# Square root and reciprocal in place of logarithm and exponential in five row norms of a two-block network

## The reference

```python
def rms_norm(x, gain):
    xf = x.astype(f32)
    y = xf * lax.rsqrt(jnp.mean(xf * xf, axis=-1, keepdims=True) + EPS)
    return (y * gain.astype(f32)).astype(x.dtype)

        h = rms_norm(x, norm_mix[l]) * (1.0 + sc_m) + sh_m      # first block, mixer
        hf = rms_norm(x, norm_ffn[l]) * (1.0 + sc_f) + sh_f     # first block, SwiGLU
    return rmsnorm(h, norm_final)                               # end of the second block
```

## Time and profile before

| what | value |
|---|---|
| runs | 4066.3, 4072.77, 4072.88 us, median 4072.77 |
| profiled execution | 4076.04 us, its span 4074.2 us |
| PE busy | 3920.8 us, 96% of the span |
| DVE busy | 2182.6 us, 54% |
| ACT busy | 814.5 us, 20% |
| POOL busy | 787.0 us, 19% |
| chain that ended last | PE 90%, DVE 4%, ACT 3%, issue 2%, DMA 1% |
| table loads at L1734 | 11 of 1283 ns |
| mean granted clock of PE | 0.987 |

### The profile page before, as it was taken

The page is one execution under the profiler, slowest core; times in us unless marked ns, Lnnn a source line. Parts: engine busy times, 40 slices in busy tenths (PEclk is TensorE's granted clock), DMA queues, the critical chain, the costliest instruction groups (busy, mean ns, idle before and its releaser), DMA issues.

```text
span 4074.2 us, 46405 instructions
## 1 busy us (share of the span) xinstructions
PE 3920.8 (96%) x17592; PEld 2913.7 (72%) x17592; DVE 2182.6 (54%) x3669; ACT 814.5 (20%) x1429; POOL 787.0 (19%) x656
## 2 busy tenths in 40 slices
PE   7999989999999999999999999999999999999998
PEld 3444478755555555665888886888789999778886
DVE  2144467534446431334556675554698888556546
ACT  2243355320100013542110101000131111110002
POOL 0038723110003100000003001130044444121300
PEclk9999999999999999999999999999999999999999
DMA  5244300012121121102332232222222222122321
GB/s 177 90 166 148 132 4 1 32 52 62 51 62 49 65 72 42 42 32 72 93 82 86 81 93 73 93 92 89 80 73 67 68 70 63 52 91 85 98 83 62
DMA packets 377174, 307.86 MB, mean 76 GB/s; under 512 B 9424, under 2 KB 345680, under 8 KB 376912
## 3 DMA queue, kind: packets, MB, share of 16 engines
q1 hardware_dynamic: 377040, 306.03, 24.1%
HBM read 303.90 MB, written 2.10 MB: 75 GB/s over the span
## 4 chain that ended last, share of the span: by engine, by line
PE 90%; DVE 4%; ACT 3%; issue 2%; DMA 1%; SPq 0%; POOL 0%; POOLq 0%; DVEq 0%; ACTq 0%
PE ps_lin L848 17%; PE ps_lin L721 10%; PE ps_lin L785 9%; PE ps_d L848 9%; PE ps_lin L1554 6%; PE ps_d L785 5%; PE ps_c L848 4%; PE ps_lin L704 4%; PE ps_d L704 3%; PE ps_lin L990 3%; PE ps_c L785 2%; PE ps_d L1340 2%; PE ps_lin L1221 2%; PE ps_lin L1208 1%; PE ps_c L704 1%
## 5 line engine op out<-in xcount | busy, mean ns | idle before, releaser
L848 PE MATMUL ps_lin<-arena,ring 128*128 128x256 f32 (+1 forms) x832 | 226.2, 425 | 1.1 <-DVE arena L2316 1.1
L3272 POOL TENSOR_TENSOR hid_in<-arena 128x256 f32<-128x256 f32 (+1 forms) x60 | 50.5, 870 | 879.9 <-PE ps_d L848 879.9
L848 PE MATMUL ps_lin<-hid_in,mixed 128*128 128x384 f32 (+1 forms) x704 | 205.4, 445 | 14.1 <-ACT hid_in L1748 13.8
L785 PE MATMUL ps_lin<-arena,ring 128*128 128x256 f32 (+1 forms) x864 | 214.1, 401 | 0.0
L2340 DVE TENSOR_TENSOR arena<-ring 128x1024 f32<-128x1024 f32 x84 | 123.0, 1464 | 168.7 <-PE ps_d L785 139.8
L721 PE MATMUL ps_lin<-mixed,ring 128*128 128x512 f32 (+1 forms) x544 | 210.4, 549 | 0.1
L3147 POOL TENSOR_TENSOR rstd<-rstd,square 128x512 f32<-128x512 f32 (+1 forms) x50 | 74.9, 1497 | 688.5 <-ACT square L1726 687.7
L848 PEld LDWEIGHTS ps_lin<-arena,ring 128*128 128x128 f32 x832 | 158.1, 190 | 64.4 <-issue 3.8
L848 PE MATMUL ps_d<-arena,mixed 128*128 128x384 f32 (+1 forms) x704 | 196.7, 432 | 0.0
L785 PEld LDWEIGHTS ps_lin<-arena,ring 128*128 128x128 f32 x864 | 164.1, 190 | 41.2 <-issue 0.2
L848 PE MATMUL ps_lin<-hid_in,arena 128*128 128x256 f32 x832 | 188.6, 380 | 3.6 <-DVE arena L2343 3.6
(11 more groups left out here) (501 smaller groups left out, 7991.1 us busy)
## 6 DMA issues: line engine op xcount, KB each, us to landing
ring<-in_ffn_w_in SPq DMA_DIRECT2D x88, 512.0 KB, 4.6
resid<-in_ada_w SPq DMA_DIRECT2D x20, 2048.0 KB, 7.9
ring<-in_mlp_w_up SPq DMA_DIRECT2D x64, 512.0 KB, 4.5
ring<-in_mlp_w_down SPq DMA_DIRECT2D x64, 512.0 KB, 4.4
ring<-in_attn_w_qkv SPq DMA_DIRECT2D x64, 512.0 KB, 4.8
ring<-in_ffn_w_out SPq DMA_DIRECT2D x32, 512.0 KB, 4.1
ring<-in_even_w_in SPq DMA_DIRECT2D x28, 512.0 KB, 5.0
ring<-in_sc_w_in SPq DMA_DIRECT2D x24, 512.0 KB, 4.9
```

Of the source, the lines that this page charges most:

```text
L785: last = mm(prod[i - 1], lhs[:, j, :], rhs(p), start=(g == j == 0), stop=(g == G - 1 and j == np_ - 1))
L848: last = mm(out, lhs[:, j, :], rhs[:, j, :], start=(j == 0), stop=(j == 3))
L3272: tt(sums[p][i], u, v, op).then_inc(s.u_hp, 1)
```

## The change

A tuple `ROOT` names the norms that are changed. For those, ScalarE loads the table of the square root ahead of its wait, takes the square root of mean + eps in one instruction that counts up `n_rs`, and is done. VectorE, once it has waited for `n_rs`, takes the reciprocal of all columns of the row in place, waits for its end, and goes on with the products as before. In mix0 this stands at the place of the old wait. "ffn0b" and "ffn1b" are not in `NORMS`; the other five of the tuple are. The six of `LATE` keep logarithm and exponential.

```diff
+ROOT = ("mix0", "ffn0", "ffn0b", "mix1", "ffn1", "ffn1b", "final")
...
             def rstd_of_norm(name, width):
-                logs()
+                act.preload_act_table(ACT.Sqrt if name in ROOT else ACT.Ln)
                 act.wait_ge(s.n_mm, MM_COUNT[name])
                 r = RS[:, 0, 0:width]
+                if name in ROOT:
+                    fn(r, psc[:, 0:width], ACT.Sqrt, bias=m["eps"], scale=1.0 / D).then_inc(s.n_rs, 1)
+                    return
                 chain(fn(r, psc[:, 0:width], ACT.Ln, bias=m["eps"], scale=1.0 / D))
...
+            def inverse(name, u, v):
+
+                dve.wait_ge(s.n_rs, NORMS.index(name) + 1)
+                chain(dve.reciprocal(RS[:, 0, u:v], RS[:, 0, u:v]))
+
             def norm(name, width, gains, strassen=None):
...
                 dve.wait_ge(s.n_rs, n + 1)
+                if name in ROOT:
+                    inverse(name, 0, width)
                 for k in range(KD):
...
             mod_scale(0, 0)
-            dve.wait_ge(s.n_rs, 1)
+            inverse("mix0", 0, T)
             for k in (0, 1):
                 scaled(k)
```

## The result

| | before | after |
|---|---|---|
| median | 4070.49 us (15 runs, 4065.58 to 4074.82) | 4078.41 us (15 runs, 4076.84 to 4080.83) |
| span of the first profiled execution | 4074.2 us | 4075.5 us |
| PE busy | 3920.8 us | 3909.9 us |
| DVE busy, instructions | 2182.6 us, 3669 | 2196.9 us, 3674 |
| ACT busy, instructions | 814.5 us, 1429 | 804.9 us, 1419 |

The ratio is 1.0021, with a 95% interval from 1.0013 to 1.0029: 7.9 us slower (by the interval, 5 to 12). The forecast was 16.1 us slower. The direction was right; the size was twice too large. A second comparison, at another time, gave 4080.86 against 4073.13 us, ratio 1.0027 (1.0017 to 1.0036).

The account below looks back on a forecast made before the run. TensorE was taken to bound the kernel; mix0 +4.2, ffn0 and mix1 +3.8 each, ffn1 +2.3, final +2.1 make +16.1 on the median 4072.77: 4088.9 us. Overall range 4065 to 4098; slow division by itself 4082 to 4104.

Parts of the forecast that it names:

- What bounds the kernel: Whole kernel: 90% of the chain that ended last lies on TensorE; an edit elsewhere counts only where TensorE stands still.
- What is removed: Table load and exponential behind the logarithm: saves 2.13 us at ffn0 and mix1, 1.69 ffn1, 1.92 final, nothing at mix0.
- The reciprocal: Added on VectorE at five norms: 7.5 ns a column, 5.91 us for 768 columns, 3.99 for 512.
- the early rows: 24 one-column reciprocals early in the run, median 164 ns, taken to mean 5.5 to 12 ns a column.
- The late one-column rows: 32 later one-column reciprocals, 153 ns, implying 1 ns a column; judged the weaker witness, as one column can hide division steps.
- mix0: First norm: reciprocal of 5.91 us pushes the next transpose, which had 1.73 us to spare: +4.2 us, nothing given back.
- It falls already with the waits of before, so a longer wait costs nothing more at four of the norms.: TensorE's granted clock after waits: no added cost at four norms; at mix0 one more low stretch would cost 2.3 us.
- One column a step: Rival: reciprocals at all five norms take 0.95 or 0.69 us, -4.6 us in all, 4068.2 us; chance 0.20.
- rival 2: Reciprocals at the five norms cost 2.5 to 5 ns a column, giving 4072 to 4081 us; chance 0.06.
- The drain: Rival: the removed table load hides a drain, so four norms each gain more than 1.283 us; 4063 us; chance 0.02.
- the load that comes back: Rival: root gets its own load behind the wait, 1.283 us at four norms, +5.1 us; 4094 or 4073 us; chance 0.02.
- The signs of being wrong: Reciprocal under 5 ns a column; TensorE's first product at ffn0 moving unlike VectorE's; clock at 0.50 longer behind longer waits.

Follow-up runs that it names:

- the three pairs of traces: The unedited kernel before and the changed kernel, each profiled three times and paired in order; spans before 4074.2, 4070.1, 4070.7 us, after 4075.5, 4078.7, 4079.7 us.
- The first pair of traces: The first profiled execution of the unedited kernel before, and that of the changed kernel; spans 4074.2 and 4075.5 us.
- the second traces of both kernels: Repeat profiles without any edit of the kernel before and the changed kernel; spans 4070.1 and 4078.7 us, medians 4071.97 and 4080.86 us.
- all fourteen traces: Three traces of the kernel before, three of the changed kernel, and one of each follow-up variant; medians of the variants run from 4049.94 to 4078.76 us.

## Why the prediction was wrong, point by point

- **What bounds the kernel.** Right. At ffn0 a delay of VectorE's first product of 2.90 us is a delay of TensorE's first matmul of 2.90.
- **What is removed.** Right within 0.1: the root costs what the logarithm did; the hop from ScalarE to VectorE is 0.10 us (root done at 881.26, reciprocal at 881.36), not 0.03. The load is worth its 1.283 us, as the kernel with only the load taken away shows.
- **The reciprocal: the term that was mis-sized.** I took 7.5 ns a column, measured are 6.26. It lies within the 5.5 to 12 of the early rows, at their lower end. On the sum that is 1.24 x 3.33 = 4.1 us: 16.1 becomes 12.0. It is the first of two steps that failed. The figure from the Trainium skill, "VectorE: DVE Perf Modes", by which a column would take an estimated 8.3 ns, is too high here; that a column of a reciprocal costs several times one of a product, the trace confirms. The late one-column rows (1 ns) were the weaker witness, as I said; that a single column hides the division's steps, no run tests. The choice of 7.5 within the bounds was a guess.
- **mix0.** +4.2 was said, and with 6.26 ns it would have been 3.3. It is 4.0, 4.6 and 3.5 in the three pairs of traces. That +4.2 lies among these is luck: the reciprocal is 0.96 us shorter than forecast, and the cover and VectorE's arrival at the row come out 0.2 to 1.4 us worse. The spare 1.73 us belongs to traces in which TensorE does the 16 products at its lower clock; one of the three has 0.56. The cover was read from a single execution.
- **"It falls already with the waits of before, so a longer wait costs nothing more at four of the norms."** This is the second step that failed. It costs nothing more: at mix1 the same matmuls from TensorE's first product on take 15.65 us in the first trace of before and 15.59 in that of after. But the time at the lower clock came to lie otherwise in four places, which gave 4.75 us back, and I had looked for a loss only: the forecast put this term at nothing. 12.9 less 4.75 is 8.2, and 7.9 was measured. The nearness is in part luck, since the three pairs of traces give back 4 to 5 us between ffn0 and final and mix0 costs 3.5 to 4.6. (The first pair of traces has 1.3 between the spans because of what the clock did ahead of ffn0, which differs by up to 4.6 us between traces of the same code.)
- **The rivals.** One column a step (0.20) is refuted by 6.26 ns, and so is rival 2, 2.5 to 5 ns (0.06), though the time measured lies in its band of 4072 to 4081. The drain is refuted by the kernel with only the load taken away, the load that comes back by the six loads left at the exponential's line. The time is inside my overall range but below the 4082 at which the forecast's own range began.
- **The signs of being wrong.** None of the three came: a column costs more than 5 ns, TensorE's first product at ffn0 moved by the same 2.90 us as VectorE's, and behind the longer wait the clock stayed low for less long, 7.9 us for 10.7. No sign was named for a clock that gives time back.

Open stays why the low stretch at ffn0 lasts 17.1 us with a wait of 9.57 us (one extra reciprocal) and 13.7 with one of 9.54 (root at ffn0 and ffn1), and by what a change at ffn0 decides how the clock falls 400 and 1800 us later. That it does is seen in traces only; the times of these kernels are too close to confirm it one by one.

## What to carry to other kernels

Before a reciprocal is moved from a row of statistics to all columns, ask for its price at that width: here 6.26 ns a column, so 768 columns cost 4.95 us to save 2.1 of table load and exponential. The load itself can go without anything in its place, if one table with both functions is asked for by name; look then also for the loads further on that this makes superfluous. And a term of a few us on TensorE's path is only as good as the clock behind it: take more than one trace, and compare windows cut from the same matmul to the same matmul.

## What the runs showed of the hardware

- VectorE's reciprocal takes 144 ns and 6.26 ns a column (4953 ns at 768, 3350 at 512, 2.90 us at 440). A single column takes 158 ns on average, which doesn't betray it: 144 + 6.26 = 150.
- On ScalarE the root of 768 columns takes the 0.90 us of the logarithm from the same operands, and the square the 0.84 us of the exponential. A table load costs 1.283 us between two instructions, with 0.03 us of gaps; without it the next product came 1.28 us earlier.
- At ffn0 TensorE's clock falls while the engine stands still and stays at the lower level for 13.7 us, in the second traces of both kernels. A wait that is 2.9 us longer covers more of this, and the same matmuls behind it take 18.1 to 18.3 us in the three traces of after, for 19.0 to 19.7 in those of before.
- The matmuls of the first down products, 400 us later, take 42.62 or 41.75 us, and those near 2700 us 51.1 or 49.4, with nothing in them changed. Which it is goes together at both places in all fourteen traces, and comes out the same in each of the three traces of either kernel.
